# A residual encoder block on one core: first-table tiles shared out anew, one-hot groups in 18 steps, seven last steps without tiles

## What is computed

```python
q = (xb @ w_q).reshape(TOKEN_BLOCK, PEER_HEADS, 2, PEER_HALF)
s1 = einsum('thd,hkd->thk', q[:, :, 0], k1)     # 128 keys in each half
s2 = einsum('thd,hkd->thk', q[:, :, 1], k2)
v1, i1 = top_k(s1, 16);  v2, i2 = top_k(s2, 16)
top_s, pos = top_k(all 256 sums v1 + v2, 16)    # expert = i1 * 128 + i2
gate = softmax(top_s)
act  = gelu(einsum('td,thkd->thk', xb, expert_u[idx]))
out  = einsum('thk,thkd->td', gate * act, expert_v[idx])
```

## Time and profile before

| | |
|---|---|
| median of three runs | 3006.27 us (3006.0 to 3010.39) |
| profiled execution, its own time | 3014.1 us |
| its span, first to last instruction | 3012.3 us |
| PE busy | 2616.7 us, 87% |
| PE weight loads (PEld) busy | 1518.2 us, 50% |
| DVE busy | 2327.7 us, 77% |
| ACT busy | 1223.7 us, 41% |
| POOL busy | 971.8 us, 32% |
| gathers' share of the 16 DMA engines | 65.3% |
| SP's transfers' share | 24.5% |

### The profile page before, as it was taken

The page is one execution under the profiler, slowest core; times in us unless marked ns, Lnnn a source line. Parts: engine busy times, 40 slices in busy tenths (PEclk is TensorE's granted clock), DMA queues, the critical chain, the costliest instruction groups (busy, mean ns, idle before and its releaser), DMA issues. The chain is left out here.

```text
span 3012.3 us, 53462 instructions
## 1 busy us (share of the span) xinstructions
PE 2616.7 (87%) x20618; PEld 1518.2 (50%) x20618; DVE 2327.7 (77%) x4875; ACT 1223.7 (41%) x3048; POOL 971.8 (32%) x888
## 2 busy tenths in 40 slices
PE   9899978787887767768888869999998997999997
PEld 7677433232332333323333326666676775766774
DVE  7965577999879899976767867767788884877776
ACT  3254143233345555533333423333244332544454
POOL 0000144444445555544343522223232222211221
PEclk9999999889997777779998989999999999999998
DMA  4113699999999999999999989999999999999995
GB/s 165 63 56 140 240 403 419 413 404 417 412 419 405 420 411 420 419 420 421 421 418 406 419 336 383 397 394 401 400 416 375 397 412 411 386 392 369 410 393 210
DMA packets 175382, 1100.76 MB, mean 365 GB/s; under 512 B 17829, under 2 KB 34341, under 8 KB 52778
## 3 DMA queue, kind: packets, MB, share of 16 engines
q0 software_dynamic: 110592, 805.36, 65.3%
q1 hardware_dynamic: 64554, 292.16, 24.5%
HBM read 1061.79 MB, written 35.65 MB: 364 GB/s over the span
## 5 line engine op out<-in xcount | busy, mean ns | idle before, releaser
L975 POOL DMA_INDIRECT arena_high<-uv_dram,idx_now x768 | 929.3, 1210 | 1665.9 <-PE ps L1258 1525.2
L2430 DVE SCALAR_TENSOR_TENSOR arena_high<-arena_low,arena_high 128x1024 f32<-128x1024 f32 x768 | 922.4, 1223 | 267.4 <-DMA arena_high<-uv_dram,idx_now 261.5
L1258 PE MATMUL ps<-arena_high 32*32 32x512 f32 x12288 | 493.5, 671 | 282.5 <-ACT arena_high L1815 278.1
L1496 PE MATMUL ps<-arena_low 128*128 128x256 f32 x2048 | 463.7, 382 | 0.0
L1496 PEld LDWEIGHTS ps<-arena_low 128*128 128x128 f32 x2048 | 384.0, 190 | 109.4 <-issue 46.0
L1806 ACT ACTIVATE gcol<-hcol 128x2 f32<-128x2 f32 x384 | 77.6, 202 | 824.4 <-DVE arena_high L2430 820.0
L1258 PEld LDWEIGHTS ps<-arena_high 32*32 32x32 f32 x12288 | 94.8, 107 | 481.6 <-ACT arena_high L1815 384.6
L1219 PE MATMUL ps<-arena_low 128*128 128x512 f32 (+1 forms) x512 | 242.0, 616 | 14.3 <-DMA arena_low<-slabs_dram 14.3
L332 PE MATMUL ps<-wv_hi_bytes,w_hi_bytes 128*128 128x512 f32 x512 | 207.6, 406 | 19.4 <-DVE v_lo_bytes L2554 13.1
L1815 ACT ACTIVATE arena_high<-arena_high,wcol 128x32 f32<-128x32 f32 x768 | 204.9, 314 | 12.5
L334 PE MATMUL ps<-wv_hi_bytes,w_lo_bytes 128*128 128x512 f32 x512 | 202.3, 395 | 0.0
(11 more groups left out here) (264 smaller groups left out, 4002.4 us busy)
## 6 DMA issues: line engine op xcount, KB each, us to landing
arena_low<-ut_dram SPq DMA_DIRECT2D x64, 1024.0 KB
arena_high<-vt_dram SPq DMA_DIRECT2D x32, 1024.0 KB, 12.7
arena_low<-vt_dram SPq DMA_DIRECT2D x32, 1024.0 KB
arena_low<-spread_dram SPq DMA_DIRECT2D x32, 512.0 KB
acts_dram<-arena_low SPq DMA_DIRECT2D x14, 1024.0 KB
arena_low<-acts_dram SPq DMA_DIRECT2D x28, 512.0 KB
arena_low<-slabs_dram SPq DMA_DIRECT2D x11, 1152.0 KB
arena_high<-uv_dram,idx_now POOLq DMA_INDIRECT x768
```

Source lines behind the costliest of these rows:

```text
L975: pool.indirect_dma_start(out=ring[:, s % RING, :], out_offset=None, in_=uv_d, in_offset=bass.IndirectOffsetOnAxis(ap=idx_now[:, s:s + 1], ...
L1258: last = nc.tensor.matmul(ps[out:out + QUAD, y_bank(t // PH) + turn, :], diag[rows, s % DIAGS, :], ring[rows, s % RING, cs], start=fresh, ...
L1496: last = nc.tensor.matmul(ps[:, 5 + n % 4 // 2, o:o + 2 * P], u_slot[n % USLOTS][:, k, :], x1T[:, BLK - DENSE:BLK, k, :], start=(k == 0), ...
L2430: last = nc.vector.scalar_tensor_tensor(out=ring[:, s % RING, 0:D], in0=x1[c][:, j, :], scalar=1.0, in1=ring[:, s % RING, 0:D], op0=ALU.mu ...
```

## The change

The first table gets 92 steps rather than 94, the second 29 rather than 31 (4.41 tiles a step), and seven last steps hold no tiles rather than three. `u_first` is now weighted: steps up to s = 55 count 133, those with groups (s = 65 to 82) 95, the others (56 to 64, 83 to 91) 193; that is 1.35, 0.96 and 1.96 tiles a step. The 64 groups take 18 steps, 3.56 a step, with four buffers for the one-hot rows rather than two, written one step ahead of their matmuls; in a step PE and ACT do groups before tiles. Slab 13 is loaded before `load_u(2)`. The first `load_g` are issued inside the loop, at tile n = 124 (`G_BACK`).

```diff
-TAIL = 3
-V_STEPS = 31
+TAIL = 7
+V_STEPS = 29
...
-G_STEP0 = PICK0 + DENSE * PH * PICK_PARTS - U0
-G_STEPS = 24
+G_STEP0 = PICK0 + DENSE * PH * PICK_PARTS - U0 + 1
+G_STEPS = 18
+HOTS = 4
 KEPT = 2
+G_BACK = G_STEP0 + G_STEPS + 4
...
+def u_share(s):
+
+    G = U0 + s
+    if G < PICK0 + 7 * STEPS:
+        return 133
+    return 95 if G_STEP0 <= s < G_STEP0 + G_STEPS else 193
+
+
 def u_first(s):
-    return NT * s // U_STEPS
+    return NT * sum(u_share(i) for i in range(s)) // sum(u_share(i) for i in range(U_STEPS))
...
-        hot = at(16, 2, 4, 2 * P)
+        hot = [at(kib, 4, 2 * P) for kib in (16, 20, 28, 32)]
...
             for n in range(NT):
+                if n == USLOTS - 2:
+                    for half in range(2):
+                        load_slab_late(LATE_SLAB + 2, half)
                 if n % 2 == 0:
                     load_u(n // 2)
-                for i in range(LATE_SLAB + 2, len(SLABS)):
-                    s0 = (i - LATE_SLAB - 3) * STEPS
-                    if n == (USLOTS - 1 if s0 < 0 else u_first(s0 + 2) + USLOTS):
+                for i in range(LATE_SLAB + 3, len(SLABS)):
+                    s0 = (i - LATE_SLAB - 3 + 32) * STEPS - U0
+                    if n == u_first(s0 + 2) + USLOTS:
                         load_slab_late(i, 0)
...
+                if n == u_first(G_BACK) + USLOTS:
+                    for c in range(2):
+                        for part in range(2):
+                            load_g(c, part)
...
-            for c in range(2):
-                for part in range(2):
-                    load_g(c, part)
...
             def dense(s):
 
-                if s == G_STEP0:
+                if s == G_STEP0 - 1:
                     for j in range(DENSE):
                         turn_picks(j)
-                if 0 <= s < U_STEPS:
-                    for n in range(u_first(s), u_first(s + 1)):
-                        u_tile(n)
                 o = s - G_STEP0
                 if 0 <= o < G_STEPS:
                     for i in range(g_first(o), g_first(o + 1)):
                         g_group(i)
+                if 0 <= s < U_STEPS:
+                    for n in range(u_first(s), u_first(s + 1)):
+                        u_tile(n)
...
-                if i >= 2:
-                    wait_again(dve, g_psum, i - 1)
+                if i >= HOTS:
+                    wait_again(dve, g_psum, i - HOTS + 1)
...
-                o = s - G_STEP0
+                o = s - G_STEP0 + 1
                 if 0 <= o < G_STEPS:
                     for i in range(g_first(o), g_first(o + 1)):
                         hot_group(i)
```

More of the change, by code:

```diff
@@ L891, in _ @@
             for n in range(NT):
+                if n == USLOTS - 2:
+                    for half in range(2):
+                        load_slab_late(LATE_SLAB + 2, half)
                 if n % 2 == 0:
                     load_u(n // 2)
-                for i in range(LATE_SLAB + 2, len(SLABS)):
-                    s0 = (i - LATE_SLAB - 3) * STEPS
-                    if n == (USLOTS - 1 if s0 < 0 else u_first(s0 + 2) + USLOTS):
+                for i in range(LATE_SLAB + 3, len(SLABS)):
+                    s0 = (i - LATE_SLAB - 3 + 32) * STEPS - U0
+                    if n == u_first(s0 + 2) + USLOTS:
                         load_slab_late(i, 0)
-                    if n == (USLOTS - 1 if s0 < 0 else u_first(s0 + 7) + USLOTS):
+                    if n == u_first(s0 + 7) + USLOTS:
                         load_slab_late(i, 1)
@@ L1508, in g_group @@
                 for q in range(4):
-                    last = nc.tensor.matmul(ps[:, (4, 7)[i % 2], q * P:(q + 1) * P], hot[:, i % 2, q, 0:P],
-                                            hot[:, i % 2, q, P:2 * P], start=True, stop=True, skip_group_check=True)
+                    last = nc.tensor.matmul(ps[:, (4, 7)[i % 2], q * P:(q + 1) * P], hot[i % HOTS][:, q, 0:P],
+                                            hot[i % HOTS][:, q, P:2 * P], start=True, stop=True, skip_group_check=True)
                 last.then_inc(g_psum.sem, 1)
@@ L2002, in dense @@
                                              ACT.Copy).then_inc(picks_ready.sem, 1)
+                o = s - G_STEP0
+                if 0 <= o < G_STEPS:
+                    for i in range(g_first(o), g_first(o + 1)):
+                        g_group(i)
                 if 0 <= s < U_STEPS:
@@ L2006, in dense @@
                             dense_act(n - 1)
-                o = s - G_STEP0
-                if 0 <= o < G_STEPS:
-                    for i in range(g_first(o), g_first(o + 1)):
-                        g_group(i)
                 v = s - U_STEPS
@@ L2520, in hot_group @@
                     wait_again(dve, picks_ready, DENSE)
-                if i >= 2:
-                    wait_again(dve, g_psum, i - 1)
+                if i >= HOTS:
+                    wait_again(dve, g_psum, i - HOTS + 1)
                 j = i // (P // 4)
                 t0 = 4 * i - j * P
-                nc.vector.tensor_tensor(hot[:, i % 2, :, 0:P], iota128[:, :].unsqueeze(1).to_broadcast([P, 4, P]),
+                nc.vector.tensor_tensor(hot[i % HOTS][:, :, 0:P], iota128[:, :].unsqueeze(1).to_broadcast([P, 4, P]),
                                         picksT[:, j, 1, t0:t0 + 4].unsqueeze(2).to_broadcast([P, 4, P]), ALU.is_equal)
@@ L2528, in hot_group @@
                     t = t0 + q
-                    last = nc.vector.tensor_scalar(hot[:, i % 2, q, P:2 * P], iota128[:, :], picksT[:, j, 0, t:t + 1],
+                    last = nc.vector.tensor_scalar(hot[i % HOTS][:, q, P:2 * P], iota128[:, :], picksT[:, j, 0, t:t + 1],
                                                    picksT[:, j, 2, t:t + 1], ALU.is_equal, ALU.mult)
```

## The result

The changed kernel takes 3060.26 us (median; 3056.79 to 3060.85), the kernel before 3008.33 in the same set: ratio 1.0168, 95% interval 1.015 to 1.0186. The forecast was 2971.7, with a range of 2950 to 2997: wrong in size and in sign. The profiled execution of after took 3056.79 us, its span 3054.7; the one of before 3014.1. The two spans are 42.4 us apart, the medians 51.9: the profiles are at opposite edges of their kernels' spread, so what follows explains the 42.4.

The account below looks back on a forecast made before the run. It took DMA at 422 GB/s to leave at most 124 us to win, with PE also near its bound. Terms -15.2 - 3.5 + 8.8 - 28.7 - 8 + 12 = -34.6 gave 2971.7 us, range 2950 to 2997.

Parts of the forecast that it names:

- step 1: s = 0 to 7: slab 13 ahead of load_u(2) removes PE's wait for it, -15.2 us.
- Step 2: s = 0 to 55: PE sets the stage and has one tile less by s = 48, -3.5 us.
- Step 3: s = 56 to 63: 16 tiles rather than 11 make the stage 65.5 us, +8.8 us.
- Step 4: s = 64 to the second table: PE and DVE stop waiting in turns, 257.5 us rather than 286.2, -28.7 us.
- no wait of tens of us on `spread_dram`: Sign that the forecast is right: no such long wait on this buffer; no size in the sum.
- The second part of step 4: s = 83 to 91: 73.5 us of PE's work, DMA 72 us for 30.4 MB, plus 2 us for the first split.
- rival B: DMA has nothing left: stages 1 to 4 keep their length, only the order changes, 3006 us; chance 0.06.
- Step 5: Second table in 29 steps: two steps of experts and 4.2 MB of gathers go, -8 us from 417.
- A: Rival: the second table gives gains back, paying for 8.4 MB inside it, 2990 us; chance 0.22.
- D: Rival: the second table speeds up and nears PE's work, some 390 us, 2953 us in all; chance 0.13.
- Step 6: Tail after the last tile: seven steps without tiles, last gathers wait for PE's experts, 42 us rather than 29.5, +12.
- Rival C: Groups in lockstep: PE waits for ACT's take-out with two PSUM banks, 12.0 us a step, 3021 us; chance 0.08.

Follow-up runs that it names:

- e5: The kernel before with only slab 13 issued ahead of load_u(2): 2993.64 us, ratio 0.9947.
- e1: The changed kernel with the gate stores (store_g) issued two places earlier in SP's loop over the first table's tiles: 3010.51 us, ratio 1.0016.
- e3: The changed kernel with store_g two places earlier and load_g back behind the whole loop of the first table: 2999.97 us, ratio 0.9982.
- e6: e1 with load_g's four transfers issued one behind each of four u pairs instead of all together: 3000.14 us, ratio 0.9981.
- e7: e3 with a tail of three steps rather than seven and 33 steps in the second table (TAIL = 3, V_STEPS = 33): 2993.01 us, ratio 0.9956.
- e10: e7 with e6's spread load_g, one transfer behind each of four u pairs: 2992.2 us, ratio 0.9959.
- e11: e7 with the gate groups in 22 steps rather than 18, which also moves tiles: 2988.67 us, ratio 0.9944.
- e12: e7 with PE's and ACT's order inside a step as before, tiles before groups: 2991.47 us, ratio 0.9958.
- e9: The kernel before with the gate groups in 18 steps (G_STEPS = 18) and nothing else: 3031.9 us, ratio 1.0087.

## Why the prediction failed

**The slab (step 1)** was right: 16.6 us in s = 0 to 7 where 15.2 were forecast, and e5 shows it alone.

**Step 2** was right: -6.8 us in the window of s = 8 to 47, where -3.5 was forecast for s = 0 to 55.

**Step 3** hit +8.8 in part by luck. In the windows the two stages split otherwise: s = 48 to 55 took 63.2 us rather than 56.4 (forecast: the same), s = 56 to 63 58.7 rather than 65.5. Those edges are DVE's marks, and PE lags behind them: at s = 64 after it had started 89 tiles of 91. From the end of PE's experts of one step to that of another, s = 48 to 55 takes 59.8 us in both kernels and s = 56 to 63 takes 65.4, just as computed, but 50.4 before rather than 56.7. By PE's marks the changes are -3.5 in s = 8 to 47 (the one tile), +15.0 in s = 48 to 63, and +39.0 rather than +48.6 from s = 64 to the second table. I had set PE's work after against DVE's window before.

**Step 4 failed**: 334.8 us where 257.5 were forecast. The step that failed is "Then DVE's own work is the bound", which gave 182 us for s = 64 to 82: ACT's wait for the gate stores was put at nothing. The sign "no wait of tens of us on `spread_dram`" was written down, but without a price or a reason; the only sentence on these stores is "What `load_g` itself waits for on SP, the last gate stores, are issued eight tiles earlier". I looked at when the last store is issued and never at when each store is issued relative to the reuse of its buffer. The runs show ACT 63.4 us at those stores in its place, and 47.2 of the stage's 77.3 us go when only they are issued earlier (e1: 287.6); 7.8 more go with `load_g` behind the loop (e3: 279.8).

Two terms could be had beforehand: a table every 2.25 steps of 9.3 us, 21 us; and the place of the store behind a tile of the next steps, at one tile a step up to 10 us by the program's order (the kernel after shows 17.9 to 36.3, since PE runs behind DVE and blocked groups hold up tiles). The third, the landing of 2.1 MB, 12 to 20 us after, is in no row of the kernel before; its nearest row was the slab's 12.7. Even that gives 22.7 us against 21. The forecast had priced a step's tiles as PE's work alone, but they also pace SP: with fewer tiles a step, everything that SP does at a tile comes later, counted in steps. The sum for the work itself was good: with the stores in time the forecast's 182 us for s = 64 to 82 compares with 186.9 (e1).

**The second part of step 4** (75.5 us from s = 83 on) stays too low even in e1 (100.7), e6 (94.4) and e3 (92.7). In e1 PE stands 15.7 us for the last pair. "behind it are the last u pair and `load_v`" was written down and costed at nothing; it was 18.54 us in the changed kernel. The larger miss is in the bytes. The forecast had 30.4 MB, 72 us, with 12.6 MB of gathers, since "the ring starts full" and nine steps would use it up in part. e3 moves 38.2 MB in this stretch, 21.7 of them gathers, at 412 GB/s; e6 38.5 MB. Nine steps use 18.9 MB of rows, so the ring filled up rather than running down, and DMA's share is 1.01 in e3 and 1.00 in e6, whichever wait stands at the end. No run takes bytes away, so that they set the length is read from the shares. In e6 PE is busy 84.78 of 94.4 us rather than 73.5: it is one step behind DVE at s = 83 (109 tiles started, so 19 are left rather than 18), and two pairs, behind waits of 3.71 and 4.03 us, take 8.83 us rather than 7.17 at a granted clock of 0.81.

**Why the repaired kernel doesn't reach 2971.7.** In s = 64 to the second table PE is busy 250.65 of 286.2 us before, and 244.65 of 287.6 in e1: nearly the same work, so only the idle time could be won, and e1 has more of it. From s = 0 to the second table, before takes 799.5 us, the slab alone (e5) 781.5, and e7, e10, e11 and e12 773.7 to 776.9; the rest of the change, repaired, is worth 5 to 8 us there. My reading, which no run tests by itself: a stretch bound by DVE (s = 65 to 82, DMA at 0.96 in e1) is followed by one bound by DMA (1.00 in e6), and work moved from one to the other is not gained, as e9 shows for DVE's groups. That is weaker than rival B: DMA has something left, but not where the work was moved.

**Step 5** was right in size: 410.5 for 409; A and D didn't come. e7 and e3 leave open how much of it is the two steps less (415.5 us with 33 steps, 415.7 with 29).

**Step 6** was under-sized by 6.5 us (48.0 rather than 41.5): the mechanism was the forecast's. PE's experts of step 379 end 16.05 us after the last tile, as forecast (16.0). Then the last two gathers, which I gave 5 us and an estimated 2 to 3 together, are issued at 3023.53 and 3025.35 and used at 3034.54 and 3036.98, 11 us or more each. The last dot product starts 30.3 us after the last tile rather than 24 (timeline of after):

```profile
3023.53 1.51 POOL L989 DMA_INDIRECT arena_high<-uv_dram,idx_now  x1 [4.51 <-PE ps L1272]
3025.35 1.98 POOL L989 DMA_INDIRECT arena_high<-uv_dram,idx_now  x1 [0.30 <-issue]
3034.54 1.22 DVE L2444 SCALAR_TENSOR_TENSOR arena_high<-arena_low,arena_high 128x1024 f32<-128x1024 f32 x1 [2.54 <-DMA arena_high<-uv_dram,idx_now]
3036.98 1.22 DVE L2444 SCALAR_TENSOR_TENSOR arena_high<-arena_low,arena_high 128x1024 f32<-128x1024 f32 x1 [1.21 <-DMA arena_high<-uv_dram,idx_now]
```

**Rival C** named lockstep, from PE's waits for ACT, at "above 11 us with PE waiting on ACT". The steps did take 208.9 / 18 = 11.6 us with PE waiting on ACT, and by that sign it would have been confirmed. The cause was another: ACT itself stood for a store. Without that wait the steps take 9.2 us with the same order and the same two PSUM banks (e1). A sign has to name the end of the chain, not its middle.

The 358 GB/s between HBM and one core of the Trainium skill (DMA: Bandwidth & Descriptors, Specifications) bound nothing in after either: two windows stand at 413 and 421. The prediction read that figure without its condition. The same page of the Trainium skill (section Bandwidth) gives about 358 GB/s for each core with both cores of the HBM domain streaming, and here one core runs. The mean over the span fell from 365 to 360 because the same bytes took longer.

## What to carry over

When a change makes a stage faster or thins out one kind of its work, list what other queues do "at" that work, and compare, for every double buffer, the time until it is filled again with issue delay plus landing: here 21 us against 18 to 36 plus 12 to 20. A store that another stage waits for belongs behind the event that fills it, not behind the progress of a neighbouring stream. Look for a wait at the end of its chain: PE's 62 us on ACT were the middle of it. And try the parts of a bundled change one by one: here one part gained 13 us, and a side effect of others lost 50.

## Unexpected of the hardware

The four gate loads (512 KB each, pieces of 1 KB) keep SP issuing for 12.07 us before and 18.65 after, and take 22.5 to 37.6 us to land after; the u pairs of 1024 KB in the same stretch take a median of 13.6. The DMA issues of after from 2440 to 2600 us (what, queue, how many, KB each, median us to landing; the fifth gate load belongs to the next stage):

```profile
arena_low<-ut_dram SPq DMA_DIRECT2D x8, 1024.0 KB, 13.6
arena_low<-spread_dram SPq DMA_DIRECT2D x5, 512.0 KB, 32.7
```

SP's next transfer, the u pair at 2558.60, is issued only then, so such loads aren't free for what stands behind them on SP. And a wait cost PE more than its length: behind the 18.54 us of idle the last pair took 9.63 us rather than 7.17, at a granted clock of 0.74 over 2583.5 to 2593.2, a mix of the levels 1.2 and 2.4 GHz.
